# First feed-forward of a hybrid decoder step: half of the key products on GpSimd, value pages issued by ScalarE, five key buffers

## The reference, cut to what matters

```python
def half_ffn(x, g, w_gate, w_up, w_down):
    h = rmsnorm(x, g)
    return x + 0.5 * ((jax.nn.silu(h @ w_gate) * (h @ w_up)) @ w_down)

def sb_weights(z, q_pos, k_pos):
    mask = k_pos[None, :] < q_pos[:, None]
    log_keep = jnp.where(mask, jax.nn.log_sigmoid(-z), 0.0)
    after = lax.cumsum(log_keep, axis=z.ndim - 1, reverse=True) - log_keep
    return jnp.where(mask, jnp.exp(jax.nn.log_sigmoid(z) + after), 0.0)

# sb_sample: z = q . k_past * 64 ** -0.5 + bias (8 heads of 64, 8192 positions, 8 samples)
#            o = einsum('bhqk,bkhd->bqhd', sb_weights(z), v_past)
# k_past = cache_k[page_table], v_past = cache_v[page_table]
```

## Time and profile before

| | us |
|---|---|
| median of three timed runs | 3218.17 |
| their range | 3209.63 to 3221.39 |
| the profiled execution, its own time | 3207.69 |
| its span in the trace | 3206.1 |
| the phase ffn1 in the trace, first to last tick of TensorE | 180.4 to 1176.1 |
| granted TensorE clock, mean over the span | 0.937 |

### The profile page before, as it was taken

How to read it: one execution, slowest core, us unless ns; L and a number is a source line. 1 busy time by engine, 2 the same in 40 slices (tenths; PEclk the granted TensorE clock), 3 DMA queues, 4 the chain that set the end, 5 groups by cost and what they waited for, 6 DMA issues and landing times. The chain is left out here.

```text
span 3206.1 us, 44833 instructions
## 1 busy us (share of the span) xinstructions
PE 2813.5 (88%) x15415; PEld 2232.8 (70%) x15415; DVE 1681.5 (52%) x2209; ACT 913.5 (28%) x1698; POOL 606.8 (19%) x821
## 2 busy tenths in 40 slices
PE   6768899999999889988778689957989999999996
PEld 4456566665665778855435588932989999999995
DVE  7559999988999953268321444332252222222223
ACT  4311111121111231089302433121143333223324
POOL 1010123223222000000220410021002333222222
PEclk8889999999999999999787799988999999999998
DMA  9966899899999511000573331133111111111111
GB/s 358 334 200 188 278 304 339 305 322 320 318 324 345 155 43 47 26 27 27 181 247 116 99 99 34 36 142 105 53 53 40 46 39 39 52 46 39 46 33 53
DMA packets 337779, 469.74 MB, mean 147 GB/s; under 512 B 26422, under 2 KB 215219, under 8 KB 336028
## 3 DMA queue, kind: packets, MB, share of 16 engines
q1 hardware_dynamic: 299748, 341.35, 32.5%
q0 software_dynamic: 37296, 125.54, 11.0%
q10 hardware_dynamic: 552, 0.57, 0.1%
HBM read 448.99 MB, written 18.39 MB: 146 GB/s over the span
## 5 line engine op out<-in xcount | busy, mean ns | idle before, releaser
L75 DVE TENSOR_TENSOR wlo<-raw,whi 128x1024 fp32r<-128x1024 f32 (+1 forms) x192 | 234.1, 1228 | 394.9 <-ACT whi L71 394.7
L98 PE MATMUL banks<-ffn_ghi,whi 128*128 128x344 f32 (+1 forms) x880 | 323.3, 367 | 67.4 <-DVE ffn_glo L1549 39.4
L1755 POOL TENSOR_TENSOR xT<-xT,ffn_down 128x344 f32<-128x344 f32 x264 | 245.2, 930 | 714.3 <-ACT ffn_down L1800 709.4
L71 ACT ACTIVATE whi<-raw 128x1024 fp32r<-128x1024 f32 (+1 forms) x192 | 197.5, 1041 | 534.1 <-PE banks L100 475.6
L98 PE MATMUL banks<-ffn_hhi,whi 128*128 128x344 f32 x1056 | 339.7, 322 | 10.1 <-DVE wlo L75 8.1
L99 PE MATMUL banks<-ffn_hlo,whi 128*128 128x344 f32 x1056 | 338.7, 321 | 0.0
L100 PE MATMUL banks<-ffn_hhi,wlo 128*128 128x344 f32 x1056 | 338.7, 321 | 0.0
L568 DVE TENSOR_TENSOR ffn_kt<-ffn_kt,ffn_q 128x1024 f32<-128x1024 f32 x256 | 311.2, 1216 | 37.1 <-DMA ffn_kt<-in_cache_k_dram 37.0
L555 POOL DMA_DIRECT2D ffn_vt<-in_cache_v_dram x384 | 206.0, 537 | 649.5 <-issue 635.1
L100 PE MATMUL banks<-ffn_ghi,wlo 128*128 128x344 f32 (+1 forms) x880 | 315.5, 358 | 0.0
L99 PE MATMUL banks<-ffn_glo,whi 128*128 128x344 f32 (+1 forms) x880 | 315.1, 358 | 0.0
(11 more groups left out here) (433 smaller groups left out, 4861.0 us busy)
## 6 DMA issues: line engine op xcount, KB each, us to landing
ffn_kt<-in_cache_k_dram SPq DMA_DIRECT2D x512, 256.0 KB, 4.3
ffn_vt<-in_cache_v_dram POOLq DMA_DIRECT2D x384, 256.0 KB, 5.1
raw<-in_w_ffn_gate_dram SPq DMA_DIRECT2D x44, 512.0 KB, 5.9
raw<-in_w_ffn_up_dram SPq DMA_DIRECT2D x44, 512.0 KB, 5.8
raw<-in_w_ffn_down_dram SPq DMA_DIRECT2D x44, 512.0 KB, 6.2
s_vt<-in_cache_v_dram SPq DMA_DIRECT2D x64, 256.0 KB, 4.3
s_vt<-in_cache_v_dram POOLq DMA_DIRECT2D x64, 256.0 KB, 4.4
a_wide<-in_w_ffn_gate_dram SPq DMA_DIRECT2D x11, 1024.0 KB, 9.9
```

The lines of the kernel that those rows point to most:

```text
L71: act.activation(self.k.whi[c % W_RING][:, 0:self.width], self.k.raw[:, c % RAW_RING, 0:self.width], ACT.Copy).then_inc(self.hi_done, 1)
L75: dve.tensor_tensor(self.k.wlo[c % W_RING][:, 0:self.width], self.k.raw[:, c % RAW_RING, 0:self.width], self.k.whi[c % W_RING][:, 0:self.w ...
L98: pe.matmul(out, whi, rhi, start=first, stop=False)
L1755: pool.tensor_tensor(x, x, dt_[:, m % DR, 0:n], ALU.add).then_inc(added, 1)
```

## The change

- by_pool(n): chunks with an odd number are multiplied by GpSimd (multiply, the same in-place product), the even ones by VectorE as before. VectorE still reduces every chunk; for an odd one it waits for a new semaphore k_times_q_pool. GpSimd's list has the 128 products and nothing else after its constants.
- The value pages are issued by ScalarE. At the head of tick t it issues as many pages as TensorE weighs at the end of tick t - 1, each behind the same wait for the used-up quad; the first eight in tick 17.
- KR is 5: five key buffers in place of four.

```diff
--- before.py
+++ after.py
@@ -467,7 +467,8 @@
 
     PAGES = 64
     KC = 2
-    KR = 4
+    KR = 5
+    POOL_EVERY = 2
     VR = 8
 
     def __init__(self, k, name):
@@ -493,6 +494,7 @@
         self.k_in = [k.sem(f"{name}_k_in{r}") for r in range(self.KR)]
         self.v_in = [k.sem(f"{name}_v_in{r}") for r in range(self.VR)]
         self.k_times_q = k.sem(f"{name}_k_times_q")
+        self.k_times_q_pool = k.sem(f"{name}_k_times_q_pool")
         self.scored = k.sem(f"{name}_scored")
         self.biased = k.sem(f"{name}_biased")
         self.kept = k.sem(f"{name}_kept")
@@ -514,6 +516,17 @@
         sp.dma_start(self.bias[:, :], self.k.a["sb_bias"].rearrange("(a n) -> a n", a=1).to_broadcast([P, NS])).then_inc(self.tables_in, 16)
         sp.wait_ge(self.tables_in, 32)
 
+    def by_pool(self, n):
+
+        return n % self.POOL_EVERY == 1
+
+    def times_q(self, eng, n):
+
+        on_pool = sum(self.by_pool(x) for x in range(n))
+        eng.wait_ge(self.k_times_q, n - on_pool)
+        if on_pool:
+            eng.wait_ge(self.k_times_q_pool, on_pool)
+
     def load_k(self, sp, n):
 
         b, c = divmod(n, 32)
@@ -521,7 +534,7 @@
             sp.wait_ge(self.scored, n - self.KR + 1)
         if c == 0:
             if b:
-                sp.wait_ge(self.k_times_q, n)
+                self.times_q(sp, n)
             sp.dma_start(self.q[:, :], self.k.qs_dram[b:b + 1, :].to_broadcast([P, 512])).then_inc(self.q_in, 16)
         for j in range(self.KC):
             at = b * self.PAGES + c * self.KC + j
@@ -548,12 +561,21 @@
         pool.wait_ge(self.consts, 11)
         pool.wait_ge(self.tables_in, 32)
 
-    def load_v(self, pool, n):
+    def load_v(self, act, n):
         if n >= self.VR:
-            pool.wait_ge(self.v_used, n // 4 - self.VR // 4 + 1)
-        page = pool.value_load(self.pages[0:1, n:n + 1], min_val=0, max_val=639)
-        pool.dma_start(self.vt[:, n % self.VR], self.values[:, ds(page, 1), :]).then_inc(self.v_in[n % self.VR], 16)
-
+            act.wait_ge(self.v_used, n // 4 - self.VR // 4 + 1)
+        page = act.value_load(self.pages[0:1, n:n + 1], min_val=0, max_val=639)
+        act.dma_start(self.vt[:, n % self.VR], self.values[:, ds(page, 1), :]).then_inc(self.v_in[n % self.VR], 16)
+
+
+    def multiply(self, pool, n):
+        b, c = divmod(n, 32)
+        r = n % self.KR
+        keys = self.kt[:, r].rearrange("p (a n) -> p a n", a=self.KC)
+        q = self.q[:, :].rearrange("p (a n) -> p a n", a=1).to_broadcast([P, self.KC, 512])
+        pool.wait_ge(self.q_in, b * 16 + 16)
+        pool.wait_ge(self.k_in[r], (n // self.KR + 1) * 32)
+        pool.tensor_tensor(keys, keys, q, ALU.mult).then_inc(self.k_times_q_pool, 1)
 
     def score(self, v, n):
         b, c = divmod(n, 32)
@@ -569,7 +591,10 @@
 
     def score_heads(self, v, n):
         c, r = n % 32, n % self.KR
-        v.wait_ge(self.k_times_q, n + 1)
+        if self.by_pool(n):
+            v.wait_ge(self.k_times_q_pool, sum(self.by_pool(x) for x in range(n + 1)))
+        else:
+            v.wait_ge(self.k_times_q, sum(not self.by_pool(x) for x in range(n + 1)))
         v.tensor_reduce(self.z[:, c * 16:(c + 1) * 16], self.kt[:, r].rearrange("p (h d) -> p h d", d=64), AX.X,
                         ALU.add).then_inc(self.scored, 1)
 
@@ -1462,12 +1487,9 @@
             @block.gpsimd
             def _(pool):
                 d.prepare(pool)
-                begun = 0
-                for t in ticks:
-                    until = min(4 * plan.quads_before(t) + d.VR, plan.WEIGHED_HERE * d.PAGES)
-                    for n in range(begun, until if t >= plan.PERIOD + 2 else 0):
-                        d.load_v(pool, n)
-                        begun = n + 1
+                for n in range(NS * plan.CHUNKS):
+                    if d.by_pool(n):
+                        d.multiply(pool, n)
 
             @block.scalar
             def _(act):
@@ -1497,7 +1519,20 @@
                     if (b := plan.weighed(t, plan.STORE)) is not None:
                         d.store(act, b)
 
+                pages = iter(range(plan.WEIGHED_HERE * d.PAGES))
+
+                def next_page():
+                    p = next(pages, None)
+                    if p is not None:
+                        d.load_v(act, p)
+
                 for t in ticks:
+                    if t == plan.PERIOD + 2:
+                        act.wait_ge(d.tables_in, 32)
+                        for _ in range(d.VR):
+                            next_page()
+                    for _ in range(4 * len(plan.quads(t - 1)) if t else 0):
+                        next_page()
                     i, at = divmod(t, plan.PER_GROUP)
                     base = i * (2 * T)
                     if at == 0:
@@ -1578,7 +1613,8 @@
                     def score_next():
                         n = next(chunks, None)
                         if n is not None:
-                            d.score(v, n)
+                            if not d.by_pool(n):
+                                d.score(v, n)
                             drain_next()
                             d.score_heads(v, n)
                             drain_next()
```

## The result

The median of 20 runs of the changed kernel is 3230.1 us (3218.5 to 3247.6), that of 20 runs of the kernel before beside it 3213.2 us (3203.5 to 3230.7): ratio 1.0046, 95% interval 1.0030 to 1.0062. It is slower by some 15 us where 58 us less were forecast. The profiled execution has a span of 3222.7 us at a mean granted clock of 0.933 (before 0.937).

The account below looks back on a forecast made before the run. TensorE was taken to lead the first feed-forward, stalling for VectorE's low parts and value pages. Terms 10 + 5 + 49 - 8 took 56 us off the stage, giving 3160 us, own range 3130 to 3195.

Parts of the forecast that it names:

- Start and end: Stage stretches without value pages: moving products off VectorE shortens TensorE's stalls by 10 us at the start, 5 at the end.
- The hold: GpSimd's product delays VectorE's 262 operations with two SBUF operands by 0.5 us each, 131 us against 146 removed.
- The pages: Value pages issued from ScalarE arrive sooner, cutting double-tick stalls by 17 x 2.6 us; 49 us gained with single quads.
- What is queued behind the pages: ScalarE's high parts come later behind page issues, harmless while VectorE is later; 8 us lost at groups' seventh ticks.
- The fifth buffer: A fifth key buffer gains nothing alone, costed at zero; it pays for the longer key cycle.
- its own signs of being wrong: GpSimd product far over 3 us, VectorE over 90% busy mid-stage, page issues over 1 us, high-part waits over 150 us.
- A: Rival: holds only 0.1 us, VectorE never leads, most stalls go and nothing is given back; 3126 us, chance 0.18.
- B: Rival: only issue time is gained, engines swap waits; 3202 us, 3215 if ScalarE is late; chance 0.23 with D.
- C: Rival: holds make VectorE the middle's bound from 0.9 us each; at 1.18 us slower, 3270 us; chance 0.17.
- D: Rival: GpSimd's product finishes after VectorE asks, 10 to 25 us of VectorE waits; counted in B, joint chance 0.23.
- stalls of two kinds: TensorE's stalls in the first feed-forward: 52 us for VectorE's low part of g, about 66 for value pages.

Follow-up runs that it names:

- e3: Changed kernel with GpSimd's product cut to 16 of each page's 512 columns, the rest left unmultiplied; ratio 0.9904 to the kernel before.
- e4: Changed kernel with each tick's value pages issued behind ScalarE's silu and high parts of that tick; ratio 1.0003 to the kernel before.
- f4: Kernel before with eleven value buffers in place of eight; ratio 0.9977 to the kernel before.
- e1: Changed kernel with all products back on VectorE, keeping five key buffers and pages on ScalarE; ratio 1.0097 to the kernel before.
- g4: Kernel before with five key buffers in place of four, nothing else; ratio 1.0009 to the kernel before.
- f3: e4 with eleven value buffers and four key buffers in place of eight and five; ratio 0.9994 to the kernel before.
- g1: Kernel before with VectorE's product of odd chunks cut to 16 of 512 columns per page; ratio 0.9904 to the kernel before.
- g2: f4 with VectorE's product of odd chunks cut to 16 of 512 columns per page; ratio 0.9782 to the kernel before.
- h2: e4 with nine value buffers in place of eight; ratio 0.9919 to the kernel before.
- e2: Changed kernel with value pages issued by GpSimd behind each tick's products, ScalarE's list as before the change; ratio 1.0154 to the kernel before.
- i1: e4 with GpSimd's product as two instructions of 128x512 in place of one; ratio 0.9916 to the kernel before.
- i3: e4 with nine value buffers and GpSimd's product as eight instructions of 128x128; ratio 0.9873 to the kernel before.

## Why the prediction was wrong

**The direction.** 56 us off the stage were summed, 15 were added. By terms:

- *Start and end, 10 + 5 us.* Measured 1 gained and 5.5 lost. The low-part ticks together stayed at 53 us. Wrong: with small products (e3) these ticks fall to 19 us, so what VectorE's relief gives there the full products take back by holds and lateness; with the pages behind the high parts (e4) 4 us of it return.
- *The hold, 0.5 us for each of 262 operations, 131 us.* Measured some 0.34 us: 82 us on the three large lines, 89 with the samples' steps. The mechanism and the operations that it hits and spares were right, the size was 1.5 times too high. The real product took 2.53 us, forecast 2.35.
- *The pages, 49 us.* The failed step, in two ways. The size: a double tick gained 0.6 us (54.6 to 43.0 us in all) and not 2.6. From the end of the matmul that frees the slots to the landing of the fourth page the 18 double ticks take, in the mean, 1.2 us to the first issue, 3.7 to the fourth and 5.2 to land before the change, 10.1 in all; after it 1.0, 3.3 and 5.2, in all 9.5. Forecast were 0.4, 3.3 and 4.3, so 8.0. So the issuing came out as forecast and the landing did not move: 4.3 us was the landing of key pages, and the 5.1 of the value pages was put down to GpSimd's queue; from ScalarE's queue they land in 5.0 as well. Why they take longer than key pages of the same size no run shows. The first issue came 0.7 us after the slots where nothing held ScalarE, and twice 2.6 and 3.6 us after, behind a high part of g for which ScalarE had waited 10 us. And one-quad ticks lost 7 us where 5 were to be gained. The worth: in f4 some 62 us of such stalls, taken away with no change to VectorE's or ScalarE's work, brought 7.
- *What is queued behind the pages, 8 us, "costs nothing while VectorE is later than that".* The second failed step. e4 against the changed kernel puts the place in the list at 14 us by both measures, and e1, without any product on GpSimd, shows the wait for high parts at 94 us against 39. The step looked at one place, g in the seventh tick, and took VectorE as the later one; VectorE is later only at the end of a tick. At its head, at the low part of the weights, it waited for ScalarE already before, and the page issues stood ahead of that. They were also longer than taken: eight pages need 8.1 us and not 6.6. The row from which 0.83 us a page was read, 1.66 us for two, spans one pitch and the second issue alone; in the same trace SP's two pages of a chunk are mostly issued 1.09 us apart, hardly faster than GpSimd's 1.15 or ScalarE's 1.06. (For four pages the error cancels: four times 0.83 is three pitches of 1.09.) The step also gave nothing for pages that are late because ScalarE is held by VectorE for over 7 us; in the trace ScalarE waits for g that long 12 times, six of them while value pages are weighed, as in the 10.05 us at 777.77. And the stall ahead of the columns, 13.9 us, was no term of the sum; it is there with the pages first and gone in e4.
- *The fifth buffer, zero.* Right (g4), as long as VectorE multiplies; f3 suggests that the rest of the change needs it.

Of its own signs of being wrong one came true, page issues over 1 us each; the wait for high parts stayed under its 150 us and VectorE's share in the middle at 80%.

**The rivals.** A fell with the holds, 0.28 to 0.47 us and not 0.1. B was the nearest: only issue time gained, waits swapped; with ScalarE late it gave 3215 where the result, on the scale of that median (3218.2 x 1.0046), is 3233. It had the right mechanisms and too small a price. The rule of the Trainium skill (Trainium Kernel Development and Optimization, Key Constraints), that issuing from several engines only saves the sequencer's issue time, agrees with the landing of 5.0 against 5.1 us; of the issue time 0.09 us a page was saved here (1.15 to 1.06). C forecast slower for another reason: at 0.9 us a hold VectorE would be the bound of the middle; its load there was 553 of 689 us. D was right in kind and near in size, 15 us of waits on VectorE.

**What the prediction missed as a whole.** It summed stalls of two kinds as if each were worth its length. With VectorE full they stand in for each other: f4 takes one kind away and the other grows by half of it. Relief of VectorE is what makes the rest worth while (g1 35 us, g2 a further 41), and of a relief of some 150 us of busy time (869 to 719 in e3) the changed kernel kept 61 (808).

**What stays open.** How the 49 us between a small and the full product split between holds and lateness exactly; why 64 products bring nothing; why value pages land later than key pages; and why h2 gains more by its times than its profiled stage shows.

## What to carry to other kernels

Before a queue is moved to another engine, look at which of that engine's results is waited for already, at the head of its list as well as at the place that bounds the stage, and put the new issues behind it. Treat two kinds of stall in one loop as alternatives until one run with each removed alone, and one with both, has shown that they add. If GpSimd is to take elementwise work with two SBUF inputs beside a busy VectorE, cut it into instructions as short as VectorE's own, and try one more buffer for what it works on.

## What the runs showed of the hardware

- A VectorE operation with two SBUF operands beside GpSimd's product of 2.53 us (128x1024) was 0.28 to 0.47 us longer in the mean in the changed kernel and up to 0.57 in other runs (e2), beside halves (1.3 us in the median) 0.14 to 0.33, beside eighths (0.46 us in the median) 0.05 to 0.12. In the other direction GpSimd's 128x512 went from 1257 up to 2375 ns. Reductions stayed at 1212 to 1218 ns throughout.
- A 256 KB value page, page number loaded and DMA issued, takes ScalarE 1.06 us, GpSimd 1.15, SP (key pages) 1.09, from one issue to the next. The value pages landed in 5.0 us from ScalarE (after) and 5.1 from GpSimd (before), key pages of the same size from SP in 4.3 (before).
- At its shortest GpSimd's product takes 2.34 us for 128x1024, 1.26 for 128x512 and 0.44 for 128x128: two halves cost 0.2 us more than the whole, eight eighths 1.2. In the mean, with VectorE beside it, it is 2.53 (after), 3.1 for two halves (i1) and 4.8 for eight eighths (i3).
